# Dense gates through a zeroed DRAM table, and key passes over four tiles each, in a one-core encoder layer

## The reference

```
q = (h @ w_q) as 8 heads x 2 halves of 128;  s = q . sub_keys      (128 keys per half)
top 16 of each half, top 16 of the 256 sums  -> experts e = i1 * 128 + i2, gates = softmax
y[t] = sum over the 128 chosen experts of gate * gelu(u[e] . h[t]) * v[e]
x = x + gate2 * RMSNorm(y)
```

## Time and profile before

| | us |
|---|---|
| median of 3 runs | 2897.84 (2889.86 to 2904.2) |
| span of the profiled execution, first to last instruction | 2847.3 |
| PE busy | 2774.5 (97%) |
| DVE busy | 2158.4 (76%) |
| POOL busy | 1313.3 (46%) |
| ACT busy | 1249.3 (44%) |
| DMA traffic over the span | 721.37 MB, 253 GB/s |

### The profile page before, as it was taken

One profiled execution on the slowest core, in us unless ns is written; L12 is line 12 of the kernel. 1 busy time (PEld: TensorE's weight loads), 2 busy tenths in 40 slices (PEclk: granted clock), 3 DMA queues, 4 the chain that ended last, 5 costly groups with the idle time before them and its releaser, 6 DMA issues.

```text
span 2847.3 us, 43522 instructions
## 1 busy us (share of the span) xinstructions
PE 2774.5 (97%) x15948; PEld 2538.1 (89%) x15948; DVE 2158.4 (76%) x3708; ACT 1249.3 (44%) x2302; POOL 1313.3 (46%) x1036
## 2 busy tenths in 40 slices
PE   6998999999999999999999999999999999999998
PEld 5776778889999999999999999999998887877786
DVE  7655545887668778678989898777768878887888
ACT  4333662233357767744454544445522233332233
POOL 0002000000000000177878887777778888888884
PEclk9998999999999999999999999999999999999999
DMA  7520223225556566589898999899999999999996
GB/s 281 227 71 31 89 75 111 69 78 177 182 177 211 200 203 205 185 286 316 301 329 301 314 303 331 308 331 311 321 361 380 359 333 345 374 341 356 341 358 262
DMA packets 328417, 721.37 MB, mean 253 GB/s; under 512 B 44000, under 2 KB 159840, under 8 KB 326368
## 3 DMA queue, kind: packets, MB, share of 16 engines
q1 hardware_dynamic: 238176, 451.18, 44.9%
q0 software_dynamic: 90112, 268.76, 27.3%
HBM read 605.50 MB, written 114.30 MB: 253 GB/s over the span
## 4 chain that ended last, share of the span: by engine, by line
PE 57%; POOL 18%; issue 5%; DVE 2%; ACT 1%; DMA 1%; DVEq 0%; SPq 0%; ACTq 0%; POOLq 0%
PE mix L1434 47%; POOL picked_act L1872 9%; POOL rows L1879 9%; PE mix L116 5%; PE sps_all L1929 2%; PE sps_all L1947 1%; PE mix L1947 1%; ACT onehot L1641 1%; PE sps_all L1521 1%; DMA rows<-in_v,eidx 0%; DVE lo L106 0%; DVE onehot L1723 0%; DMA wq_raw<-in_w_q 0%; DVEq L1123 0%; ACT hi L101 0%
## 5 line engine op out<-in xcount | busy, mean ns | idle before, releaser
L1872 POOL DMA_INDIRECT picked_act<-act_early,aidx x384 | 467.0, 1216 | 1043.0 <-PE mix L1434 938.5
L1434 PE MATMUL mix<-a_hi,hi 128*128 128x320 f32 (+1 forms) x3072 | 810.1, 318 | 2.0 <-DVE lo L106 1.9
L1434 PE MATMUL mix<-a_lo,hi 128*128 128x320 f32 (+1 forms) x3072 | 808.8, 317 | 0.0
L1434 PE MATMUL mix<-a_hi,lo 128*128 128x320 f32 (+1 forms) x3072 | 808.5, 317 | 0.0
L1879 POOL DMA_INDIRECT rows<-in_v,eidx x512 | 651.3, 1272 | 166.4 <-issue 133.2
L1782 DVE SCALAR_TENSOR_TENSOR ys<-rows,coef,ys 128x1024 f32<-128x1024 f32 x504 | 633.9, 1284 | 118.6 <-DMA rows<-in_v,eidx 105.3
L106 DVE TENSOR_TENSOR lo<-raw,hi 128x1024 fp32r<-128x1024 f32 x384 | 469.2, 1222 | 301.4 <-ACT hi L101 301.0
L101 ACT ACTIVATE hi<-raw 128x1024 fp32r<-128x1024 f32 x384 | 404.8, 1054 | 358.3 <-PE mix L1947 348.3
L1434 PEld LDWEIGHTS mix<-a_hi,hi 128*128 128x128 f32 x3072 | 533.6, 188 | 3.2 <-ACT gelu L1650 2.3
L1434 PEld LDWEIGHTS mix<-a_lo,hi 128*128 128x128 f32 x3072 | 535.1, 188 | 0.0
L1434 PEld LDWEIGHTS mix<-a_hi,lo 128*128 128x128 f32 x3072 | 534.7, 188 | 0.0
(11 more groups left out here) (268 smaller groups left out, 3899.3 us busy)
## 6 DMA issues: line engine op xcount, KB each, us to landing
raw<-in_u SPq DMA_DIRECT2D x256, 512.0 KB, 4.9
raw<-in_v SPq DMA_DIRECT2D x128, 512.0 KB, 6.0
act_late<-gelu SPq DMA_DIRECT2D x128, 320.0 KB, 4.6
act_in<-act_late SPq DMA_DIRECT2D x128, 256.0 KB, 6.5
act_early<-gelu SPq DMA_DIRECT2D x128, 192.0 KB, 1.8
gate_d<-free_lo SPq DMA_DIRECT2D x19, 1024.0 KB, 8.1
gt<-gate_d SPq DMA_DIRECT2D x64, 256.0 KB
free_lo<-gate_d SPq DMA_DIRECT2D x64, 256.0 KB, 7.6
```

The source lines that it names most:

```text
L1434: done = pe.matmul(dst, w, a[:, k, cols], start=first, stop=last)
L1872: pool.indirect_dma_start(out=g.picked_act[:, e:e + 1], out_offset=None, in_=act_tables[e // (EARLY * CHOSEN)], in_offset=bass.IndirectOff ...
```

## The change

The first and last tiles swap places: the gathered tiles are now 4 to 7 (`GATHERED_TILES`), the dense ones 0 to 3. `EARLY` is 4, so each key pass has four tiles in one part of 512 columns, and all gathered activations come from the first pass.

One-hots, compares, weighing, gate products, their PSUM copies, `gate_d` and its loads are gone. A DRAM table `act_gates` holds, for each expert, 512 activations and beside them 512 gates. SP stores zeros over the gates' half at the start of the attention. POOL then writes each chosen gate with an indirect DMA of 128 single values (`scatter_gates`), 16 per head and tile, 512 in all, before its picks. As a later head can choose the same expert, DVE first adds the earlier heads' gates of that expert (`sum_repeats`), and the heads of a tile are written in order. Dense tiles 0 to 2 have their top-k in the retrieval, tile 3 in the first key pass. The second pass stores its activations into the other half; the dense pass loads both halves with one DMA of 512 KB a step, and DVE multiplies them. Rows are now due at 21 per 10 steps in the key pass and 2 a step in the dense pass.

```diff
-EARLY = 3
+EARLY = 4
 GATHERED = 4
+GATHERED_TILES = tuple(LATE + s if s < EARLY else DENSE + s - EARLY for s in range(GATHERED))
-HEAD_TILES = EARLY
+HEAD_TILES = DENSE - 1
+HEAD_GROUP = 2
+HEAD_EXPS_AT = (7, 11, 15)
+SUMS_IN_RETRIEVAL = {2: (1,), 4: (2,), 5: (3,)}
+EARLY_SUMS = [(h, c) for h in (1, 2, 3) for c in range(HEAD_TILES)]
+SUMS_FROM, SUMS_EVERY = 9, 2
+LATE_SUMS = [(h, c) for h in range(4, HEADS) for c in range(HEAD_TILES)]
+LAST_SUMS_FROM = 47
-TOPK_ORDER = (1, 2, 3, 4, 0)
+TOPK_ORDER = tuple(t - HEAD_TILES for t in (HEAD_TILES, *GATHERED_TILES))
...
+AG = 2 * DTOK
+ZERO_TILES = 64
+DENSE_FROM = 2 * N - 8
-ROW_EVERY = (5 / 12, 7 / 12)
+ROW_EVERY = (10 / 21, 1 / 2)
...
+        g.act_gates = nc.dram_tensor("act_gates", (NKEYS, P, AG), F32, kind="Internal").ap()
...
         @block.sync
         def _(sp):
+            sp.wait_ge(g.zeros_ready, 1)
+            for j in range(N // ZERO_TILES):
+                for t in range(DENSE):
+                    cols = slice(DTOK + t * P, DTOK + (t + 1) * P)
+                    tables = g.act_gates[j * ZERO_TILES:(j + 1) * ZERO_TILES, :, cols].rearrange("n p c -> p n c")
+                    sp.dma_start(tables, g.zeros[:].unsqueeze(1).to_broadcast([P, ZERO_TILES, P])).then_inc(g.zeros_stored, 16)
             for done in g.early_sems:
                 sp.sem_clear(done)
             sp.wait_ge(queries_done, 2)
             sp.wait_ge(keys_done, 2)
             for n in range(WO_AHEAD):
                 sp.dma_start(g.wo_raw[n][:], i["w_out"][:, MIX_ORDER[n], :]).then_inc(g.wo_in[n], 16)
...
         @block.gpsimd
         def _(pool):
+            pool.memset(g.zeros[:], 0.0).then_inc(g.zeros_ready, 1)
...
+def finish_heads(g, dve, b):
+
+    gates = g.gates_d[:, 0:HEAD_TILES, group_heads(b), :]
+    norm = g.norm[:, 0:HEAD_TILES * HEAD_GROUP].rearrange("p (c h) -> p c h", h=HEAD_GROUP)
+    dve.wait_ge(g.heads_exps, b + 1)
+    dve.tensor_reduce(norm, gates, AX, ALU.add)
+    for h in range(HEAD_GROUP * b, HEAD_GROUP * (b + 1)):
+        dve.scalar_tensor_tensor(g.sidx[:, 0:HEAD_TILES, h, :], g.chosen_r[:, h, :, :, 1], float(NKEYS), g.chosen_r[:, h, :, :, 0],
+                                 ALU.mult, ALU.add)
+    dve.drain()
+    dve.reciprocal(norm, norm)
+    for c in range(HEAD_TILES):
+        slots = g.sidx[:, c, group_heads(b), :]
+        dve.tensor_scalar(slots, slots, float(AG), g.gate_col[:, c:c + 1], ALU.mult, ALU.add)
+    dve.drain()
+    dve.tensor_tensor(gates, gates, norm.unsqueeze(3).to_broadcast([P, HEAD_TILES, HEAD_GROUP, TOPK]), ALU.mult)\
+       .then_inc(g.scatter_ready, 1)
...
+def sum_repeats(g, dve, t, h):
+
+    before = h * TOPK
+    full = [P, TOPK, before]
+    same = (g.repeats if (h, t) in EARLY_SUMS else g.repeats_late)[:, 0:TOPK * before].rearrange("p (a b) -> p a b", b=before)
+    earlier = lambda a: a[:, t, 0:h, :].rearrange("p h k -> p (h k)").unsqueeze(1).to_broadcast(full)
+    dve.drain()
+    dve.tensor_tensor(same, g.sidx[:, t, h, :].unsqueeze(2).to_broadcast(full), earlier(g.sidx), ALU.is_equal)
+    dve.drain()
+    dve.tensor_tensor(same, same, earlier(g.gates_d), ALU.mult)
+    dve.drain()
+    dve.tensor_reduce(g.repeated[:], same, AX, ALU.add)
+    dve.drain()
+    dve.tensor_tensor(gate_sums(g, t, h), g.repeated[:], g.gates_d[:, t, h, :], ALU.add).then_inc(g.summed, 1)
...
-    rows = 12 * (min(m, late) - ROWS_FROM + 1) // 5
-    return min(GATHERED * CHOSEN, rows + max(0, m - late) * 12 // 7)
+    rows = 21 * (min(m, late) - ROWS_FROM + 1) // 10
+    return min(GATHERED * CHOSEN, rows + max(0, m - late) * 2)
...
+def load_act_gates(g, sp, n):
+
+    sp.dma_start(g.ag_in[n % ACTS][:], g.act_gates[n]).then_inc(g.ag_in_sem[n % ACTS], 16)
...
     if m < N:
-        parts = [(acc[:, 0:EARLY * P], slice(0, EARLY * P))]
+        parts = [(acc[:, 0:EARLY * P], slice(LATE * P, S))]
+    elif LATE * P <= HALF:
+        parts = [(acc[:, 0:LATE * P], slice(0, LATE * P))]
...
-            sp.dma_start(g.act_late[m - N], g.gelu[m % GELUS][:]).then_inc(g.act_stored[m % GELUS], 16)
+            sp.dma_start(g.act_gates[m - N][:, 0:DTOK], gelu[:, 0:DTOK]).then_inc(stored, 16)
...
     def coefficients(n):
         if n >= 2:
             dve.wait_ge(g.clo_ready, n - 1)
...
+        dve.wait_ge(g.ag_in_sem[n % ACTS], 16 * (n // ACTS + 1))
+        both = g.ag_in[n % ACTS]
+        dve.tensor_tensor(g.cf[n % 2][:], both[:, 0:DTOK], both[:, DTOK:], ALU.mult).then_inc(g.cf_ready, 1)
...
+    def scatter_gates(t, head):
+        if head:
+            pool.wait_ge(g.scattered[t], 16 * TOPK * head)
+        for k in range(TOPK):
+            pool.indirect_dma_start(out=gate_table, out_offset=bass.IndirectOffsetOnAxis(ap=g.sidx[:, t, head, k:k + 1], axis=0),
+                                    in_=gate_sums(g, t, head)[:, k:k + 1], in_offset=None)\
+                .then_inc(g.scattered[t], 16)
+
+    for head in range(HEADS):
+        if head == 0:
+            pool.wait_ge(g.zeros_stored, 16 * DENSE * N // ZERO_TILES)
+            pool.wait_ge(g.scatter_ready, 1)
+        for t in range(HEAD_TILES):
+            if head:
+                pool.wait_ge(g.summed, (head - 1) * HEAD_TILES + t + 1)
+            scatter_gates(t, head)
+    pool.wait_ge(g.scatter_ready, HEADS // HEAD_GROUP + 1)
+    for head in range(HEADS):
+        if head:
+            pool.wait_ge(g.summed, HEAD_TILES * (HEADS - 1) + head)
+        scatter_gates(HEAD_TILES, head)
     act_complete(N - 1)
```

More of the change, by code:

```diff
@@ L1227, in token_numbers @@
         dve.tensor_scalar(g.token_col[:, s:s + 1], g.token_col[:, 0:1], float(s % EARLY * P), None, ALU.add)
+    for t in range(DENSE):
+        dve.tensor_scalar(g.gate_col[:, t:t + 1], g.token_col[:, 0:1], float(DTOK + t * P), None, ALU.add)
 def topk_turn(m):
@@ L1233, in topk_turn, with stores_of, acts_stored @@
     return (x, at) if m >= TOPK_FROM and x < TOPK_TILES else (None, None)
[L1236 to L1280 removed]
+def stores_of(m):
+    return 1 if m < N or LATE == DENSE else 2
+def acts_stored(last, s):
+    return 16 * sum(stores_of(m) for m in range(s, last + 1, GELUS))
 def rows_by(m):
@@ L1505, in retrieval_vector @@
                 split_ahead(2 * h + 5)
+            if stage == 4 and h and h % HEAD_GROUP == 0:
+                finish_heads(g, dve, h // HEAD_GROUP - 1)
+            if stage == 4:
+                for earlier in SUMS_IN_RETRIEVAL.get(h, ()):
+                    for c in range(HEAD_TILES):
+                        sum_repeats(g, dve, c, earlier)
             head_stage(g, dve, h, stage)
+        if h % HEAD_GROUP == HEAD_GROUP - 1:
+            shift_heads(g, dve, h // HEAD_GROUP)
     dve.wait_ge(g.s_out, QTILES)
@@ L1548, in gathered_steps @@
             if m == last_row_at(s) + (1 if s < GATHERED - 1 else -3):
+                if s == 0:
+                    for t in range(DENSE):
+                        sp.wait_ge(g.scattered[t], 16 * CHOSEN)
                 if s < GATHERED - 1:
@@ L1759, in first_tiles @@
         if m == HEADS_LAST:
-            shift_topk(g, dve, g.gates_r, g.tops_r[:].rearrange("p c h k -> p (c h) k"), HEAD_TILES * HEADS)
+            shift_heads(g, dve, HEADS // HEAD_GROUP - 1)
         if m == HEADS_LAST + 2:
-            norm_topk(g, dve, g.gates_r, HEAD_TILES * HEADS, 0)
-            for c in range(HEAD_TILES):
-                last = chosen_rows(g, dve, c, g.chosen_r[:, :, c])
-            last.then_inc(g.chosen_ready, 1)
+            finish_heads(g, dve, HEADS // HEAD_GROUP - 1)
+        step, odd = divmod(m - SUMS_FROM, SUMS_EVERY)
+        if odd == 0 and 0 <= step < len(LATE_SUMS):
+            sum_repeats(g, dve, LATE_SUMS[step][1], LATE_SUMS[step][0])
+        step, odd = divmod(m - LAST_SUMS_FROM, SUMS_EVERY)
+        if odd == 0 and 0 <= step < HEADS - 1:
+            sum_repeats(g, dve, HEAD_TILES, step + 1)
     def add_row(e):
@@ L1823, in sweeps_vector @@
         first_tiles(m)
-        x, batch = gate_turn(m - 1)
-        if x is not None and batch < 0:
-            take_slots(x)
-        elif x is not None:
-            add_gate_low(x * GATE_BATCHES + batch)
-        if gate_batch(m + 2) is not None:
-            compare(gate_batch(m + 2))
         topk_steps(m)
@@ L1953, in dense_product @@
             done.then_inc(g.tile_done, 1)
-    def key_steps(m):
-        expert_product(g, pe, m)
-        x, batch = gate_turn(m)
-        if x is not None and batch < 0:
-            transpose_slots(x)
-        elif x is not None:
-            gates(x * GATE_BATCHES + batch)
-    m = 1
-    while m < 2 * N:
-        rounds = key_rounds(m)
-        if rounds < 2:
-            key_steps(m)
-            m += 1
-            continue
-        with pe.Fori(0, rounds) as q:
-            for step in range(m, m + ROUND):
-                expert_product(g, pe, step, ROUND * q)
-                if gate_batch(step) is not None:
-                    gates(gate_batch(step), ROUND // GATES_EVERY * q)
-        m += rounds * ROUND
+    expert_product(g, pe, 1)
```

(7 more changed lines are left out.)

274 lines of the change are left out of this document (81 added, 193 removed).

## The result

The change makes the kernel slower: 3384.33 us (3361.26 to 3401.28, 4 runs) against 2900.55 us for the kernel before (2889.86 to 2904.2, 4 runs), a ratio of 1.1682 with a 95% interval of 1.1624 to 1.174. I had predicted 3000 us, 2822 to 3075.

A forecast was written before the change was run, and what follows sets the result against it. PE and POOL were both taken as full, with POOL's gathers deciding. First pick at 1374 plus 1549 of gathers plus 28 gave a span of 2951, 104 slower; 2897.8 + 104 gave 3002, rounded 3000 us, range 2822 to 3075.

The forecast's parts named there:

- the scatters: First key pass: 512 POOL DMAs from 568 us, 1.40 us each, done at 1301, hidden ahead of the picks.
- Rival (d): POOL before the picks: scatters cost much more than gathers; at 2.2 us they end at 1710, near 3338; chance 0.07.
- The gathers set the end: From the first pick at 1374: 1024 POOL gathers, 1.44 then 1.59 us each, 1549 us; last leaves at 2923.
- rival (a): From 1374 on: POOL keeps up and PE sets the pace; span 2786, median 2837 us; chance 0.2.
- The zeros: Attention: eight 4 MB stores ahead of w_out's loads make mix_out start 47 us late; bounds 0 and 156 us.
- The row of the packets: Two score stores of 512 B packets, 26.5 ns each; gave 109 us for the zeros and the 47 us delay.
- Retrieval and late sums: DVE: added sums and gate finishes cost 3 us in the retrieval (bounds 0 and 20), 0 in the first pass.
- The zero point: Sum: median of the runs lies 50.5 us above the 2847.3 span; 2897.8 + 104 gives 3002, rounded 3000.

The follow-up runs named there:

- A: Kind of chip, told by the kernel before, which took 2852 to 2856 us on it.
- B: Kind of chip, told by the kernel before, which took 2884 to 2902 us on it; the change was first measured there.
- reads: The change with its 512 scatters made indirect gathers out of v into a tile nobody reads: 2985.27 us on A, 3370.27 us on B.
- the table by tokens: The change with its scatters into another DRAM table, one 64 KB row per token: 2982.59 us on A, 3388.69 us on B.
- part 3: Reruns on B: the change 3359.88 us, no scatters 3016.13, table by tokens 3388.69, spread scatters 3127.81; also a count of semaphore records in the traces.

## Why the prediction was right or wrong

**The step that failed** is that of the scatters: I costed their own time, found it hidden (done at 1301, "with 73 us to spare"), and gave PE nothing for it. Their own time was right. A scatter takes 0.96 us and 0.30 between two; on A the last starts at 1321.6:

```profile
L1877 POOL DMA_INDIRECT gates_t<-sums_last,sidx x112: 952/958/1503, 1154.6 to 1321.6; - x112
```

On B it starts at 1463.7 in the change, since sums come late from a DVE that PE keeps waiting. What was missing is their effect on another engine. The text gave the scatters' duration a range, and their effect on PE none. On B that effect is 344 us: from 700 to 1400 us PE makes 1915 matmuls with the scatters and 3073 without. On A the nothing that I put down fits: reads and the table by tokens, with 512 such DMAs each, take no longer than no scatters. The change itself was never run on A.

**Rival (d)** had the sign and nearly the size (3338 us), but by luck, with another mechanism: 2.2 us for a scatter and picks that wait for POOL. In the change the picks wait for PE: POOL's wait ahead of the first pick is 293.8 us.

```profile
POOL picked_act L1852 <- PE mix L1467: 305.8, 27, 293.8
```

**The gathers set the end: right.** Where PE isn't held up, the intervals came out within 0.02 us of the forecast. The kernel without scatters on A, its last row and its rates in the second key pass and twice in the dense pass (busy, count):

```profile
L1856 POOL DMA_INDIRECT rows<-in_v,eidx x512: 932/948/2030, 1413.6 to 2955.2; - x171
```
```profile
1700.00:2000.00 300.00, 237.22 (x207) 0.97 0.91 314
2200.00:2500.00 300.00, 242.99 (x188) 0.99 0.92 333
2600.00:2900.00 300.00, 241.86 (x191) 1.00 0.93 340
```

300 / 207 = 1.45 us (forecast 1.44), 300 / 188 = 1.60 and 300 / 191 = 1.57 (forecast 1.59). The first pick came 22 us after my 1374, the average gather took (2955.2 - 1395.9) / 1024 = 1.523 us (forecast 1.513), the span is 2988.7 (forecast 2951): 22 us from the later first pick, 10 from the gathers, 6 from the end. So rival (a), PE sets the pace, is out, and the rise of about 5% on A is this term and the next. That the first pick's place costs is what the run without scatters, with three tiles and later zeros, bears out: its first pick comes 178 us sooner than without scatters alone, and its time is 130 us shorter.

**The zeros: right.** The wait ahead of the output projection, after and before:

```profile
PE otp L1041 <- PEq L687: 54.5, 1, 54.5
```
```profile
PE otp L1030 <- PEq L683: 3.7, 1, 3.7
```

51 us against the 47 forecast. SP needs 100.4 us to issue the eight stores, and the loads of w_out come behind. The estimate from the Trainium skill's formula (DMA: Bandwidth & Descriptors, Anatomy of one DMA) was a delay of 17 us; the page fits it to DMAs that GpSimd issues, and these are issued by SP. The row of the packets was nearer, and the measurement decides.

**Retrieval and late sums: a little low.** Without scatters on A the expert product starts at 686.3, 64 after the earlier trace rows; 51 are the zeros, so 13 where I took 3 (bounds 0 and 20).

**The zero point: wrong.** I added the 50.5 us between the profiled span of before and the median of its runs as if they were overhead. Each run lies less than 2 us above its own span. The kernel before again: a span of 2845.3 goes with a time of 2847.14 us, on A. By these numbers the trace I argued from is of kind A, the times beside it of kind B. A trace from A couldn't show what B does, but the gap of 1.7% was a question that I left unasked.

## What to carry to other kernels

A stream of indirect DMAs from POOL need not be free for the engines that it doesn't share data with. Hiding 512 of them in a pass where POOL was idle cost 344 us of 3360 on one kind of chip and nothing that shows on another, in runs that were all profiled; in the trace it looks like PE idle on "issue" with DMA, DVE and ACT idle too. So spread such DMAs (4.4 for each tile step of 5.5 us got back two thirds), ask for their count first, run the changed kernel itself beside its variants on the same chip, time it once without the profiler, count the records before you trust an "issue", and be wary when a profiled span and the median of runs differ by more than the runs do.

## What I had not expected of the hardware

- On chips of kind B, POOL's indirect DMAs of 128 x 4 bytes at one in each 1.25 to 1.27 us, read or write, leave PE a matmul in about each 2.5 us (40 in 100 us); at one in 3 to 4 us PE loses nothing that I can see; at 4.4 in about 5.5 us it loses 15% of its matmuls in that pass (2624 of 3073). On kind A there is no loss at 1.27 us. What in the chip does it, and how the two kinds differ, isn't shown: the number of packets, how long a packet of the scatters takes (a median of 13 ns on both kinds), the address patterns tried and a transfer of instructions are excluded. The recording of semaphore updates, which falls behind on B as soon as indirect DMAs run closely, is the rival that stands (part 3).
- The holes begin some 25 us after the stream does (first scatter 577.8, holes from about 600) and end when a longer DVE operation or a late sum breaks it. My reading of the timelines, which no run tested by taking DVE's part away, is that they keep themselves going: a starved PE leaves DVE idle, and beside an idle DVE POOL's scatters come at their least period.
- Without scatters the expert product (with its weight loads) still waits 123.6 us for issue on B and 20.1 on A, beside the gathers at one in 1.5 us. The kernel before may lose its 50 us in the same way; no trace of it on B was taken.
